# An earlier wait for the PSUM turns of a decoder step, and two modulation products moved behind the output projection

## What is computed

```
mod = silu(c) @ w_ada + b_ada            # 6 x 1024: shift, scale, gate, twice
h   = rms_norm(x) * (1 + scale_m) + shift_m
u, q, k, v, z_pool, z_att = split(h @ w_in)
A   = pool_mix(u) @ w_proj_pool          # windows 2, 4, 8, 16
B   = attention, 3 dilated groups merged by their denominators @ w_proj_att
x   = x + gate_m * rms_norm((sigmoid(z_pool)*A + sigmoid(z_att)*B) @ w_out)
h   = rms_norm(x) * (1 + scale_f) + shift_f
x   = x + gate_f * rms_norm((gelu(a) * b) @ w_down),  a, b = conv3(h @ w_up)
```

## Time and profile before

| | |
|---|---|
| median of three runs | 1026.33 us |
| profiled execution | 1025.8 us, of it span 1024.0 us |
| PE busy | 1000.2 us (98%) |
| DVE, ACT, POOL busy | 472.9, 387.4, 112.4 us |
| granted TensorE clock, mean | 0.994 of full speed |
| HBM | 302 GB/s over the span |

### The profile page before, as it was taken

How to read it: one execution, slowest core, us unless ns; L and a number is a source line. 1 busy time by engine, 2 the same in 40 slices (tenths; PEclk the granted TensorE clock), 3 DMA queues, 4 the chain that set the end, 5 groups by cost and what they waited for, 6 DMA issues and landing times.

```text
span 1024.0 us, 21045 instructions
## 1 busy us (share of the span) xinstructions
PE 1000.2 (98%) x8961; PEld 972.0 (95%) x8961; DVE 472.9 (46%) x846; ACT 387.4 (38%) x633; POOL 112.4 (11%) x175
## 2 busy tenths in 40 slices
PE   7999999999999999999999998999999999999996
PEld 6899999999999999998989998999999999999996
DVE  6633324322542253325856448566555565532233
ACT  5334423432343234432113346454454544322132
POOL 1000300040004000324913000000000000000000
PEclk9999999999999999999999999999999999999998
DMA  9966486757666777439995672666666666666412
GB/s 319 316 237 207 154 262 234 243 174 250 230 241 210 254 253 248 154 94 362 368 313 202 216 263 73 203 225 223 222 220 223 226 217 199 192 216 189 123 46 84
DMA packets 218410, 222.34 MB, mean 217 GB/s; under 512 B 6429, under 2 KB 173725, under 8 KB 217533
## 3 DMA queue, kind: packets, MB, share of 16 engines
q1 hardware_dynamic: 218233, 220.85, 64.4%
q10 hardware_dynamic: 84, 0.15, 0.0%
HBM read 213.56 MB, written 96.03 MB: 302 GB/s over the span
## 4 chain that ended last, share of the span: by engine, by line
PE 84%; POOL 4%; DVE 4%; SPq 3%; DMA 2%; issue 2%; ACT 1%; DVEq 0%; ACTq 0%; POOLq 0%
PE acc L1514 73%; POOL cached L702 3%; SPq L403 2%; PE psT L1723 2%; PE psT L1736 1%; PE acc L1605 1%; PE psT L1750 1%; PE psS L1706 1%; PE psS L1563 1%; DMA ada_first<-in_w_ada 1%; POOL tha L709 1%; DVE w_lo L1010 1%; PE psT L1595 1%; PE psS L1704 1%; DMA qB<-sample_qkv 1%
## 5 line engine op out<-in xcount | busy, mean ns | idle before, releaser
L1514 PE MATMUL acc<-act_hi,w_hi 128*128 128x260 f32 x1856 | 380.3, 286 | 1.9 <-DVE w_lo L1010 1.3
L1514 PE MATMUL acc<-act_hi,w_lo 128*128 128x260 f32 x1856 | 373.6, 283 | 0.0
L1514 PE MATMUL acc<-act_lo,w_hi 128*128 128x260 f32 x1856 | 373.0, 282 | 0.0
L1010 DVE TENSOR_TENSOR w_lo<-raw,w_hi 128x1024 fp32r<-128x1024 f32 (+1 forms) x148 | 185.1, 1252 | 319.3 <-ACT w_hi L728 318.9
L1514 PEld LDWEIGHTS acc<-act_hi,w_hi 128*128 128x128 f32 x1856 | 285.4, 188 | 8.8 <-issue 5.4
L1514 PEld LDWEIGHTS acc<-act_hi,w_lo 128*128 128x128 f32 x1856 | 285.8, 188 | 0.0
L1514 PEld LDWEIGHTS acc<-act_lo,w_hi 128*128 128x128 f32 x1856 | 285.6, 188 | 0.0
L728 ACT ACTIVATE w_hi<-raw 128x1024 fp32r<-128x1024 f32 (+1 forms) x148 | 154.7, 1047 | 142.5 <-PE acc L1514 133.4
L1514 PE MATMUL acc<-g_hi,w_hi 128*128 128x260 f32 x352 | 71.6, 284 | 0.0
L1514 PE MATMUL acc<-g_hi,w_lo 128*128 128x260 f32 x352 | 70.8, 282 | 0.0
L1514 PE MATMUL acc<-g_lo,w_hi 128*128 128x260 f32 x352 | 70.7, 282 | 0.0
(11 more groups left out here) (286 smaller groups left out, 989.5 us busy)
## 6 DMA issues: line engine op xcount, KB each, us to landing
out_k_sample<-in_cache_k_w SPq DMA_DIRECT2D x89, 368.0 KB
out_v_sample<-in_cache_v_w SPq DMA_DIRECT2D x89, 368.0 KB
raw<-in_w_in SPq DMA_DIRECT2D x60, 512.0 KB, 9.1
raw<-in_w_up SPq DMA_DIRECT2D x44, 512.0 KB, 5.5
ada_last<-in_w_ada SPq DMA_DIRECT2D x12, 1024.0 KB, 9.4
ada_first<-in_w_ada SPq DMA_DIRECT2D x16, 512.0 KB, 7.4
raw<-in_w_down SPq DMA_DIRECT2D x16, 512.0 KB, 4.8
out_k_sample<-in_cache_k_w SPq DMA_DIRECT2D x16, 511.0 KB
```

Of the source, the lines that this page charges most:

```text
L1010: dve.tensor_tensor(w_lo[PLACE[n]][:, 0:cols], raw[:, n % RAW, 0:cols], w_hi[PLACE[n]][:, 0:cols].bitcast(F32), ALU.subtract).then_inc(lo_ ...
L1514: ins_ = pe.matmul(acc[b][:, half, 0:HALF], w, x[:, t, half * HALF:(half + 1) * HALF], start=first and i == 0 and j == 0, stop=last and i ...
```

## The change

Three places. First, the three waits for `o_lod` on PE become waits for `o_joined`. Second, PE makes `OADA+10` behind the fourth late fold and `OADA+11` behind the second `turn_normed`, and no longer behind `up` (1,0); SP issues the last four `w_ada` fills together behind the `w_up` fill (1,1), where the last two stood behind fill (2,0) and its cache copies. Third, ACT's wait for `us_ready` and the copy of the samples' high part stand between `act_hi[0]` and `un[0]`.

```diff
@@ SP
-                    if (i, h) in ((1, 1), (2, 0)):
-                        ada_load(OADA + 8 + 2 * (i - 1))
-                        ada_load(OADA + 9 + 2 * (i - 1))
+                    if (i, h) == (1, 1):
+                        for s in range(OADA + 8, OADA + 12):
+                            ada_load(s)
@@ ACT
                     act.activation(act_hi[:, k, 0:TP], psN[0], ACT.Identity, bias=b, scale=a).then_inc(act_ready, 1)
+                    if k == 0:
+                        act.wait_ge(us_ready, 5)
+                        act.activation(act_hi[:, :, TP:TC], small[:, :, :], ACT.Copy).then_inc(us_hid, 1)
                     if k >= 4:
                         act.wait_ge(act_split, 8 + k - 3)
                     act.activation(un[:, k % 4, :], psN[0], ACT.Identity, bias=b, scale=a).then_inc(xn_taken, 1)
                 else:
                     act.wait_ge(u_ready, k // 2 + 1)
                     act.activation(act_hi[:, k, 0:TP], un[:, k % 4, :], ACT.Copy).then_inc(act_ready, 1)
-                if k == 0:
-                    act.wait_ge(us_ready, 5)
-                    act.activation(act_hi[:, :, TP:TC], small[:, :, :], ACT.Copy).then_inc(us_hid, 1)
@@ PE, turn_weights, turn_kv, and behind unit pp 1
-                    pe.wait_ge(o_lod, p)
+                    pe.wait_ge(o_joined, p)
...
-                    pe.wait_ge(o_lod, p)
+                    pe.wait_ge(o_joined, p)
...
-                        pe.wait_ge(o_lod, PAIRS)
+                        pe.wait_ge(o_joined, PAIRS)
@@ PE, between out and up
             late_ada(OADA + 9)
             late_fold(3)
+            late_ada(OADA + 10)
...
             turn_normed(0)
             turn_normed(1)
+            late_ada(OADA + 11)
@@ PE, up
                     if (i, half) == (1, 0):
                         pe.wait_ge(u_ready, KT // 2)
                         late_fold(LATE - 2)
-                        late_couple(LATE - 1)
```

## The result

The changed kernel takes 1021.0 us (median of 4 runs, 1020.41 to 1022.29), the kernel before 1026.47 in the same comparison: ratio 0.9948, 95% interval 0.9932 to 0.9963. That is faster by 5.5 us. The forecast was 4.0 us under 1026.33, at 1022.3, with a range of 1020.9 to 1024.4. The sign and the range hold, the range by 0.1 us; the forecast time is 1.3 us too high, and the experiments are mostly about that difference.

What follows compares the result with a forecast made beforehand. PE bounds the kernel, busy 98% of the span, so time counts if taken from its queue. Gains 1.92 + 1.89 + 0.18 = 3.99, about 4.0 us: 1026.33 - 4.0 = 1022.3 us, 8-in-10 range 1020.9 to 1024.4.

Steps and rivals of the forecast that it cites:

- Part 1: Turns in pairs 1 to 3 wait for the joined output: gains 0.45, 1.03 and 0.44, sum 1.92 us.
- release of 0.15 us: Pairs 1 and 3: time from DVE's end to PE's start, used to place the scores behind the modulation add.
- the full 2.94: Rival to part 1: scores not held by `ada_out`, so the turns gain 2.94 us, time 1021.3; chance 0.10.
- Part 2: Last couple's 64 matmuls leave PE's queue behind up (1,0), hidden in two waits before the up products: gain 1.89 us.
- Part 3: Samples' high part copied before `un[0]`: first `act_lo` and the stage 0.18 us earlier; bounds -0.2 and +0.66.
- The short wait at L1612: Sign of part 3: a new short PE wait on DVE `act_lo` L1093 for the second tile.
- a second low stretch: Clock rival: low clock on the first up units after the change, costing 1.5 us, time 1023.8; chance 0.08.
- The row 618 to 620 with the clock at 1.00: Evidence against the clock rival: PE did eight transposes only there, yet the clock stayed at 1.00.
- The late fill: Slower rival: `OADA+10` lands late before the first `turn_normed`; needs a 25 us landing, time 1028.5; chance 0.03.
- the even point of 621.8: Late-fill rival: landing time of `OADA+10` at which the change turns from faster to even.

Runs made afterwards that it cites:

- old couple: Changed kernel with the last couple of products back behind up (1,0) and its two fills in their old place; 1023.86 us, ratio to before 0.9971.
- old couple, filler of the right size: Changed kernel, couple and fills in their old places, plus unused matmuls of the moved groups' size (32 records) in each of the two waits; 1023.16 us.
- old couple, filler too large: Changed kernel, couple and fills in their old places, plus unused matmuls (64 records) in each of the two waits; 1024.08 us, ratio to before 0.9981.
- old turns: Changed kernel with its three PE waits on the low part (o_lod) again; 1022.99 us, ratio to before 0.9962.
- old samples: Changed kernel with ACT's copy of the samples' high part behind un[0] again; 1020.78 us.
- old fills: Changed kernel with the last two w_ada fills behind the fill (2,0) and its cache copies again; 1021.47 us, ratio to before 0.9950.
- bias first: Changed kernel with DVE's modulation add of pairs 1 and 3 ahead of its wait for the high part; 1019.91 us, in a second comparison 1019.32 us.

## Why the prediction was right, and where it was short

**All profiles together.** One line for each profile: where the 1.2 GHz stretch lay between 600 and 630 us, and how long the first turn of the scaled rows to the fold behind up (1,0) took.

```
                                        low stretch     turn to fold
before, first trace                      609 to 613        22.66
before, second                           620 to 624        23.99
before, third                            620 to 624        24.06
old couple                               617 to 621        23.49
old couple, filler of the right size     606 to 610        22.42
old couple, filler too large             none              23.16
changed, first trace                     none              22.41
changed, second and third                607 to 611, 605 to 610     22.41, 22.41
old turns                                none              22.42
old samples                              none              22.68
old fills                                606 to 610        23.44
bias first, two traces                   604 to 609, 605 to 609     22.41, 22.42
```

With PE standing in both waits, the clock fell on the up units in 3 of 4 profiles. With work in them, it did in none of 10. Part of this could be where an earlier low stretch happens to lie, since no profile has two ahead of its last few us. Without the profiles with an early one it is 3 of 3 against none of 4 (changed first, old turns, old samples, filler too large). One of the four, the larger filler, keeps the couple behind up (1,0), which speaks for the work in the waits and against the work taken from there; it is one profile. No run put work into only one of the two waits.

The record has more: the mean granted clock of the executions that were timed for the comparisons, most of them without a kept trace. An estimate: the stretch of 3.4 us at half clock takes 0.0017 off the mean of an execution of 1024 us. The traces without such a stretch have means of 0.995 and 0.996, those with one 0.993 to 0.995; the rest of the difference lies in the last few us, where the clock is low in every trace.

```
mean granted clock        executions   0.991 to 0.992   0.993 to 0.994   0.995 to 0.996
kernel before                     48               22               23                3
old couple                        10                0                9                1
the two fillers                   23                0               14                9
changed kernel                    15                0                5               10
```

The fillers reach 0.995 in 9 of 23, the two kernels with empty waits in 4 of 58. That bears out the work in the waits, with the limit that the mean does not tell where the clock was low. It shows something else too: in 22 of 48 executions the kernel before lost more clock than in any kept trace (all three have 0.994). These 22 took 1027.2 us on average, the other 26 took 1025.8. No trace shows where that further low stretch lies, and none of the 10 executions with the old couple alone had it.

**Part 1** said 1.92 us with an `ada_out` wait in pairs 1 and 3. The mechanism is as written, in the pairs named, and absent in pair 2. The traces give 1.68 to 1.8. The term that was off is the release of 0.15 us: from the end of `mod` to the scores it took 0.25 (169.18 to 169.43), which is most of why pairs 1 and 3 gave 0.32 each and not 0.45. That the gain would be the full 2.94 was a rival; moving the add showed that it could be had (2.97 us from scores 0 to 3).

**Part 2** said 1.89 us; it measured 2.10. I had taken the length of the 64 records and left out the 0.2 us between the fold and their start at 641.77, which goes with them: the next unit now starts 0.03 us behind the fold. The fold in the trace of before:

```profile
641.57 0.27 PE L1947 MATMUL psT<-ident,ada_rows 128*128 128x128 f32 x1
```

Both groups were hidden, with 0.44 us left in the first wait (0.37 forecast). The fills were in time.

**Part 3** said 0.18 us; it measured 0.25 to 0.27. PE came 0.45 us earlier to the first pass and kept a little over half of it. The short wait at L1612 that was to show it is not in the profile's list.

So the sum of the forecast, 4.0, was right to 0.1 us for the pair of executions that it was made for, and that is in part luck: part 1 came out 0.24 us smaller, parts 2 and 3 larger by 0.21 and 0.07. The range held by luck too: its edge was 1020.9, and the two later medians of the changed kernel, 1020.57 and 1020.86, lie just outside it. **The step that failed is the one that carried it over to the median.** I took the profiled execution to be like the others but for 0.5 us, and the clock to be a risk of the change: that a second low stretch might fall on the up units after it, at 1.5 us. The price was about right (1.1 to 1.4). The side was wrong: the low stretch fell there in the kernel before, in two of three profiles, and in none of the changed kernel. The row 618 to 620 with the clock at 1.00, which I read as a sign that no stretch comes there, was from the one trace where it had just come and gone. The Trainium skill, page "TensorE: Matmul & The Clock Gate", section "What's actually happening", says that the window in which the chip watches TensorE's activity runs free of the kernel. The profiles agree in this: the same program had its low stretch at 609 once and at 620 twice, with the start of the work (the first turn of the scaled rows, 618.91, 618.26 and 618.54) moved by less than 1 us.

4.0 and 1.3 for the clock make 5.3; the medians gave 5.5, 6.1 and 6.1 (1026.91 - 1020.86) in three comparisons, the means of the same runs 5.2, 6.1 and 5.3. **Open** is what is left, up to some 0.8 us. The first candidate is again the clock, in the 22 executions of the kernel before that lost more of it than any trace shows. Another is the samples' attention: from the last scores to its first turn, executions differ by 1.0 us. The three of the changed kernel took 0.2 to 0.6 us less there than the first trace of before, the other two of before 0 and 0.35 more. But the kernel with the old turns, which has the same instructions as the kernel before up to there, took 0.55 less, and the first with the moved add 0.3 more. I can't tie it to an edit.

**The late fill**, the rival on the slower side, did not come: the four fills took 7.2 us in the median to land, against the 25 it would have needed. (One figure of that rival was wrong: by its own rule a landing at 626 is 4.2 us past the even point of 621.8, which makes 1030.5 and not 1028.5.)

## What to carry to other kernels

Work moved into an engine's wait can be worth more than its own length if the engine is TensorE: here 1.1 to 1.4 us more in an execution in which the clock had fallen over the dense products that follow. When one profile of a kernel shows a low-clock stretch at a place where it costs nothing, take a second and a third before pricing a change on the first; the mean granted clock of the runs told without a trace that the kernel before loses more (under 0.993 in 22 of 48, in none of 15 after). And when a wait on PE is relaxed, look at the next wait behind it in the same queue, and at what stands in front of its producer: a 0.2 us add in the queue behind the relaxed step cost two fifths of the gain, and moving it into DVE's idle time gave 1.3 us more.

## What the runs showed of the hardware that was not expected

The granted clock fell to its lower level for about the same time, from 3 to 4 rows of 1 us, wherever it fell in this part of the kernel, and once or not at all in each of the 14 traces; the means of 22 executions of the kernel before are too low for once. A pair of matmuls of 260 columns took 0.64 us in it against 0.40. Behind the row sums it cost nothing, since DVE's update of 4.87 us sets the time there. An f32 matmul leaves two records in the trace. A release from DVE to PE took 0.15 us in one place (170.23 to 170.38) and 0.25 in another (169.18 to 169.43). The span before the first pair's scores differs by 1.5 us between executions of the same instructions (63.93 to 65.47 over the profiles).
